# First norm of a two-layer encoder trunk: the order of square root, transposes, copies and gate weights at the start of the program

## The reference, cut to what matters

```python
def rmsnorm(x, g):
    xf = x.astype(jnp.float32)
    y = xf * lax.rsqrt(jnp.mean(xf * xf, axis=-1, keepdims=True) + EPS)
    return (y * g.astype(jnp.float32)).astype(x.dtype)

def layer(x, norm_g, w_in, ...):
    h = rmsnorm(x, norm_g)
    proj = h @ w_in
    qa, ka, va, gfl, gbl, za, qb, kb, vb, zb, ma, mb = jnp.split(proj, split_points(), axis=-1)
    ...
    return x + merged @ w_out
```

## Time and profile before

| what | us |
|---|---|
| median of 3 runs | 2059.89 |
| lowest and highest | 2059.82, 2060.16 |
| the profiled execution, whole | 2061.01 |
| its span in the trace | 2059.1 |
| PE busy in that span | 1967.9 (96%) |

### The profile page before, as it was taken

How to read it: one execution, slowest core, us unless ns; L and a number is a source line. 1 busy time by engine, 2 the same in 40 slices (tenths; PEclk the granted TensorE clock), 3 DMA queues, 4 the chain that set the end, 5 groups by cost and what they waited for, 6 DMA issues and landing times.

```text
span 2059.1 us, 37278 instructions
## 1 busy us (share of the span) xinstructions
PE 1967.9 (96%) x13184; PEld 1817.1 (88%) x13184; DVE 987.4 (48%) x1397; ACT 919.0 (45%) x1816; POOL 736.1 (36%) x744
## 2 busy tenths in 40 slices
PE   5998999999999998999999989999999999989997
PEld 4988999999999997887799889999999999978786
DVE  4112555569755654324241045557686555633224
ACT  4213445533556665422441145545336656643233
POOL 3433222248432331333553332222682332323244
PEclk9999999999999999999999999999999999999999
DMA  4321222432121114331432121225221111152323
GB/s 146 93 59 42 73 60 66 139 102 65 37 65 46 56 46 145 111 117 62 126 98 77 51 57 62 66 69 158 81 58 47 46 61 53 54 175 71 118 87 138
DMA packets 122923, 168.92 MB, mean 82 GB/s; under 512 B 15696, under 2 KB 89296, under 8 KB 122832
## 3 DMA queue, kind: packets, MB, share of 16 engines
q1 hardware_dynamic: 82656, 107.52, 18.3%
q10 hardware_dynamic: 40176, 60.18, 8.5%
HBM read 136.19 MB, written 31.46 MB: 81 GB/s over the span
## 4 chain that ended last, share of the span: by engine, by line
PE 86%; DVE 5%; ACT 4%; issue 2%; ACTq 1%; DMA 1%; POOL 0%; DVEq 0%
PE ps L578 11%; PE ps L579 11%; PE ps L580 11%; PE ps L540 10%; PE ps L542 10%; PE ps L541 10%; PE ps L708 5%; PE ps L723 3%; PE ps L764 3%; PE ps L661 2%; PE ps L779 2%; PE ps L780 2%; PE ps L729 2%; PE ps L752 1%; PE ps L753 1%
## 5 line engine op out<-in xcount | busy, mean ns | idle before, releaser
L1336 POOL TENSOR_TENSOR w_lo<-w_raw,w_hi 128x256 fp32r<-128x256 f32 (+1 forms) x560 | 586.8, 1055 | 1254.6 <-ACT w_hi L915 1252.8
L578 PE MATMUL ps<-w_hi,act_hi 128*128 128x256 f32 x2112 | 611.6, 290 | 13.8 <-POOL w_lo L1336 8.6
L580 PE MATMUL ps<-w_hi,act_lo 128*128 128x256 f32 x2112 | 598.5, 283 | 0.0
L579 PE MATMUL ps<-w_lo,act_hi 128*128 128x256 f32 x2112 | 598.4, 283 | 0.0
L915 ACT ACTIVATE w_hi<-w_raw 128x256 fp32r<-128x256 f32 (+1 forms) x560 | 275.7, 501 | 515.1 <-PE ps L542 300.7
L578 PEld LDWEIGHTS ps<-w_hi,act_hi 128*128 128x128 f32 x2112 | 405.0, 192 | 19.9 <-POOL w_lo L1336 9.4
L579 PEld LDWEIGHTS ps<-w_lo,act_hi 128*128 128x128 f32 x2112 | 405.4, 192 | 2.7
L580 PEld LDWEIGHTS ps<-w_hi,act_lo 128*128 128x128 f32 x2112 | 405.2, 192 | 0.0
L540 PE MATMUL ps<-w_hi,o_hi 128*128 128x512 f32 x384 | 157.6, 410 | 9.3 <-DVE o_lo L1507 6.9
L542 PE MATMUL ps<-w_hi,o_lo 128*128 128x512 f32 x384 | 152.1, 396 | 0.0
L541 PE MATMUL ps<-w_lo,o_hi 128*128 128x512 f32 x384 | 151.7, 395 | 0.0
(11 more groups left out here) (174 smaller groups left out, 3574.2 us busy)
## 6 DMA issues: line engine op xcount, KB each, us to landing
w_raw<-in_w_in SPq DMA_DIRECT2D x352, 128.0 KB, 2.1
proj<-stg ACTq DMA_DIRECT2D x36, 768.0 KB, 3.5
w_raw<-in_w_in SPq DMA_DIRECT2D x80, 256.0 KB, 2.7
w_raw<-in_w_out SPq DMA_DIRECT2D x64, 256.0 KB, 2.7
w_raw<-in_w_branch_a SPq DMA_DIRECT2D x32, 256.0 KB, 2.7
w_raw<-in_w_branch_b SPq DMA_DIRECT2D x32, 256.0 KB, 2.7
q<-proj ACTq DMA_DIRECT2D x8, 768.0 KB, 4.9
zb<-proj ACTq DMA_DIRECT2D x8, 768.0 KB, 9.7
```

The source lines that it names most:

```text
L578: mm(out, act_hi[:, k, tok], w_hi[:, k % RING, 0:BGW], start=(k == 0 and t % 2 == 0), stop=False, skip_group_check=True)
L579: mm(out, act_hi[:, k, tok], w_lo[:, k % RING, 0:BGW], start=False, stop=False, skip_group_check=True)
L580: last = mm(out, act_lo[:, k, tok], w_hi[:, k % RING, 0:BGW], start=False, stop=(k == KT - 1), skip_group_check=True)
L1336: G.tensor_tensor(w_lo[:, slot, 0:width], w_raw[:, slot, 0:width], w_hi[:, slot, 0:width].bitcast(F32), ALU.subtract).then_inc(s.w_lo_done, 1)
```

## The change

Four edits, all of them at the start of the program, before the loop over the layers:

1. ACT takes the root directly behind the squares of tiles 0 to 2; the gate weights come behind the fourth copy `turn_hi`.
2. ACT makes all six `turn_hi` in a row (with the gate weights in between), then the three splits, then the squares of tiles 3 to 5 in a row.
3. The first six transpose steps use four banks: tile 0 banks 4 and 5, tile 1 banks 2 and 3, tile 2 banks 4 and 5 (`FIRST_BANKS`).
4. The steps of tiles 1 and 2 wait for a `turn_free` that is lower by two (`spare=2`). Tile 1 is thereby free from the start, and tile 2 waits for the `turn_lo` of tile 0.

The norm of the second half and of the second layer keep their banks and their order; `normed_tokens` only takes its banks as a tuple now.

```diff
+FIRST_BANKS = 4, 2, 4
...
-            def turn_normed(t, half, base):
+            def turn_normed(t, half, base, spare=0):
...
-                turn_step(hn[:, t % NH, half * HALF:(half + 1) * HALF], half, base)
+                turn_step(hn[:, t % NH, half * HALF:(half + 1) * HALF], half, base, spare)
...
-            def turn_step(src, m, base=6):
-
-                pe.wait_ge(s.turn_free, at("turn_free"))
+            def turn_step(src, m, base=6, spare=0):
+
+                pe.wait_ge(s.turn_free, at.peek("turn_free", 1 - spare))
+                at.skip("turn_free", 1)
...
             for t in range(NH):
                 for half in range(2):
-                    turn_normed(t, half, 4)
+                    turn_normed(t, half, FIRST_BANKS[t], 2 if t > 0 else 0)
...
-            gate_weights()
             rsqrt_seed(NH)
+            for t in range(NH):
+                for half in range(2):
+                    turn_hi(act_hi, half, t, half * 4, FIRST_BANKS[t])
+                if t == NH - 2:
+                    gate_weights()
             for k in range(SKEW):
                 split(k - SKEW)
             for t in range(NH):
-                for half in range(2):
-                    turn_hi(act_hi, half, t, half * 4, 4)
                 act.wait_ge(s.x_in[NH + t], 16)
                 sum_squares(NH + t)
...
-                        turn_lo(act_hi, act_lo, [(half, t)], half * 4, base)
+                        turn_lo(act_hi, act_lo, [(half, t)], half * 4, bases[t % NH])
...
-            normed_tokens(0, 4)
+            normed_tokens(0, FIRST_BANKS)
```

More of the change, by code:

```diff
@@ L1521, in normalise, with normed_tokens @@
                     dve.sem_inc(s.passed, 1)
-            def normed_tokens(first, base):
+            def normed_tokens(first, bases):
                 normalise(first)
@@ L1801, in _ @@
             dve.sem_inc(s.group_free, 2)
-            normed_tokens(0, 4)
+            normed_tokens(0, FIRST_BANKS)
             for layer in range(DEPTH):
                 rank_gates(0)
-                normed_tokens(NH, 2)
+                normed_tokens(NH, (2,) * NH)
                 first_features(0)
@@ L1868, in _ @@
                 if layer + 1 < DEPTH:
-                    normed_tokens(0, 4)
+                    normed_tokens(0, (4,) * NH)
                 else:
```

## The result

| | median us | runs | lowest to highest |
|---|---|---|---|
| before, beside the change | 2060.02 | 4 | 2059.82 to 2060.34 |
| changed | 2048.20 | 4 | 2045.21 to 2050.81 |
| changed, in a second comparison | 2048.41 | 4 | 2047.77 to 2049.19 |
| before, beside that | 2060.24 | 15 | 2058.85 to 2061.07 |

The ratio is 0.9942, 95% interval 0.9925 to 0.9959: 11.8 us faster, in the second comparison 11.8 us too. The forecast was a gain of 9.85 us and a time of 2050.0; its range, 2046.9 to 2052.2, holds the measured 2048.20. With 15 runs the kernel before spreads over 2.2 us too, so the narrow 0.5 us of its first runs was chance.

The account below looks back on a forecast made before the run. The prediction took PE (86%) as the bound, with its first instruction waiting for DVE's `hn`. Root 7.93 plus banks and copies 1.9 gave 9.85 us with rounding, from 2059.89 to 2050.0, range 2046.9 to 2052.2.

Parts of the forecast that it names:

- The root: Program start: earlier table load gains 5.00 us, faster small DVE steps 2.10, shorter first `hn` tile 0.83; together 7.93.
- the rival built on a waiting switch: At the root's table load behind an accumulator read: the switch waits up to 1.28 us, giving 2051.3; chance 0.07.
- The banks and the row of copies: First transpose to gates' first matmul: 7.1 us instead of 8.99, since PE need not wait for banks; gain 1.9.
- Splits and squares moved: Behind the copies on ACT: costs nothing if PE finds its weights; covers of 4.0, 4.4 and 3.4 us.
- The rival of the starved weights: First features: block 4's load lands too late and PE waits, slower than before from 20.4 us landing; chance 0.02.
- The clock: Behind the gates' start: low stretch of 6.1 us kept; ending a few us earlier or later is worth -1.3 to +0.4.
- the clock rises in the 24 transposes: Before the gates: PE's clock rises and the pause does not lower it, 2.7 us more gain, 2047.3; chance 0.28.
- the rival's second half: Between transposes and gates: the pause of some 1.8 us does not lower PE's clock again; whole rival's chance 0.28.
- The sum: Whole kernel: 7.93 + 1.9 = 9.85 us with rounding, all at the start, median from 2059.89 to 2050.0.

Follow-up runs that it names:

- the second profile: The changed kernel run again word for word, against the kernel before: 2048.41 us, ratio 0.9941.
- the square of experiments: Against the kernel before: root alone 2052.68 us; root and four banks without ACT's new order 2051.85; root and new order with two banks 2052.03; banks alone 2058.37.
- the pair with fillers there: Kernel before and changed kernel, each plus 28 identity transposes at two later PE waits per layer, none at the start: 2053.76 and 2041.52 us.

## Why the prediction was right, and where it was off

**The root, 7.93 us: right, 7.83 measured.** Load of the table at 10.66 (forecast 10.59), small steps of 0.17, first tile at 13.35 (13.28), first transpose at 14.74 (14.64). The experiment with the root alone adds that only 7.1 of it reach the gates without the new order. The drain that the Trainium skill, page "ScalarE: Activation LUTs", section "What ACT_TABLE_LOAD costs", adds to a switch did not show: the load starts 0.01 us behind the read of the accumulator (10.46 + 0.19) and takes 1.28. The measurement decides, and the rival built on a waiting switch falls.

**The banks and the row of copies, 1.9 us: right, 2.1 measured.** First copy at 15.86 (15.77), fourth at 18.42 (18.32), gate weights at 18.91, gates at 21.61 (21.7). The prediction gave the gain to banks and order together; the square of experiments says that each needs the other for half of its worth.

**Splits and squares moved: at no cost, right.** PE never waits for `w_lo` in the first half's features. The rival of the starved weights did not come.

**The clock: the term that was mis-sized.** The forecast took a low stretch of 6.1 us behind the gates' start for both kernels. In the changed kernel it ended 3.7 us behind that start, in the second profile 3.5. From 9.95 the lead grows by that to 11.2 us. The prediction had the condition in a rival: the clock rises in the 24 transposes. It did, in both profiles, but the rival's second half failed, since the pause of 2.2 us lowered it again. What came, 1.2 us of additional gain, lies inside the forecast's own allowance of -1.3 to +0.4 for that stretch. With the pause filled, the rival's case came true at the start: 13.0 us ahead of the kernel before at 168 us, where the rival gave 12.6.

**The sum, 9.85 us: 2.0 short.** 1.2 of that is the start's clock and 0.1 the gates' start itself. The other 0.7 is what the four later steps leave, three of about 1 us and one of 2.3, which the prediction did not see at all: it had the lead pass to the end one for one. In the profiled pair these steps leave 1.3, and without the shorter issue of `zb` they would have taken some 0.5 away. So it is partly luck that the total came this near to the forecast: the later steps, which it left out, happen to cancel for the most part. That the balance differs between executions is what the spreads show. That the steps near 190 and 1195 come from the clock is shown: they are gone in the pair with fillers there. Near 810 it is argued from the windows, and most of the last step is the DMA issue on ACT's queue.

## What to carry to other kernels

Where PE is the bound and its first instruction waits, the chain ahead of it counts in full, and it can be read to 0.1 us from the timelines: a transfer that stands ahead of a root only by the order of one engine, and small vector steps that POOL's work stretches sevenfold, were 7 of the 10 us. Order and buffers have to be changed together: each brought only about half of its worth without the other. Count low clock as a cost of PE's waits: here it followed waits of 2.2 and 3.5 us, and some cheap transposes in them were worth 7 us of 2048, as much as the root. And don't look for a lead of 1 us in the total; follow it from place to place in the trace.

## What the runs showed of the hardware

- The granted clock fell with PE at work in part: 24 transposes up to 19.4, a pause of 2.2 us, and at 22.0, 0.4 us behind the gates' start, it read 0.50 (in the second profile at 21.6, with that start). Sixteen transposes of 0.12 us in that pause kept it at 1.00.
- The column of the granted clock reads 1.00 ahead of the first recorded change even where matmuls run at the low level: the earlier trace rows has 19 matmuls in 6.04 us, the 1.2 GHz pace, at 1.00. The distance between matmul starts is what tells the level there.
- A delay of 1 us at the start of a kernel of 2048 us did not make the median longer (2047.6 against 2048.4), and a gain of 1.8 us at the start did not show in the total either (2048.3).
- A DMA issue on ACT's own queue holds ACT back for as long as the issue lasts, and the same one did not always last equally long: 2.1 to 4.2 us for the fourth load of `zb` in the second layer, over all profiles. ACT's next copy started 0.05 to 0.06 us behind its end (at 1825.84 and 1814.30).
